# The router of a product-key expert layer: a second search over 112 sums in place of 256

## The chip, the cores and the metric

One Trainium2 chip, one of its cores. The metric is the time of one launch on the device in microseconds (us), the median over runs.

## The reference

One step of a one-layer decoder: attention and pooling, then an expert layer with product keys (PEER). The change touches only the choice of experts. For each of 1056 tokens (in 9 tiles of 128) and each of 8 heads:

```python
q = (hb @ w_pq).reshape(t, PEER_HEADS, 2, PEER_HALF)
s = jnp.einsum('thpk,hpnk->thpn', q, peer_keys).astype(jnp.float32)
sv, si = lax.top_k(s, PEER_TOPK)                        # 2 x (16 of 128 keys), sorted
cand = sv[:, :, 0, :, None] + sv[:, :, 1, None, :]      # 16 x 16 sums
cidx = si[:, :, 0, :, None] * N_KEYS + si[:, :, 1, None, :]
fv, fi = lax.top_k(cand.reshape(t, PEER_HEADS, 256), PEER_TOPK)
e = jnp.take_along_axis(cidx.reshape(t, PEER_HEADS, 256), fi, axis=-1)
g = jax.nn.softmax(fv, axis=-1)
```

The 16 experts `e` of a token and head are then evaluated and summed with the weights `g`.

## The kernel before

The program is a row of blocks, each with its own code for TensorE, VectorE, ScalarE, GpSimd and the DMA queue SyncE, and with a barrier of all engines at its end. `router` is such a block, and it is run twice: for the first 2 token tiles (names that begin with `t0`) amid the attention, and for the other 7 tiles (`t2`) after it. T is the number of tiles, and token is the partition. After the early router the kernel goes on with attention; after the late one `gate_matrix` spreads the gates, and a long stage of dense experts follows.

Inside a router the engines work through 8 heads. `heads` writes head 0 and head 7 out and rolls heads 1 to 6 into a loop. The parts of a head:

- ScalarE and GpSimd split the query weights of each half into a high and a low part (lines 1314 and 1364). GpSimd's split waits for ScalarE's.
- TensorE forms the queries in three products (lines 1276 to 1278) as soon as GpSimd's split is there, and with the keys the scores (line 1285). ScalarE copies both out (lines 1321 and 1329).
- VectorE finds the 16 best of each half (`top16`), writes the 256 sums (line 1439) over the scores, and finds the 16 best of these, again with `top16`. That function makes five passes over all the rows it is given: MAX8 (line 1409), FIND_INDEX8 (1413), MATCH_REPLACE8 (1417), MAX8 (1422), FIND_INDEX8 (1426); the find and replace passes have a MATCH_VALUE_LOAD before each. Between passes `settled` waits for the pass and copies one column (line 1403).
- VectorE then subtracts the best sum (line 1446), turns the place found (`at`, 0 to 255) into its row (shift by 4, line 1450) and column (and with 15, line 1451), casts both to float (1453), and compares each with 0 to 15 (line 1458, twice; the second comparison follows at once).
- GpSimd picks the key numbers by these comparisons: a multiplication (line 1380) and four halving sums (line 1386), for each half. In GpSimd's order of head m stand the two next splits and then the picks of head m-1. VectorE may cast the indices of head m (line 1438) only when the picks of head m-1 are done.
- ScalarE takes the exponential (line 1351) of head m-1 in the midst of head m; VectorE sums it, inverts it and writes the gates (lines 1462, 1464, 1466), which ends its head.

At the end VectorE forms the expert numbers for the gathered tiles (line 1473), and TensorE and ScalarE turn the picks of the others.

Of the kernel before, what the change touches and what calls it, by code (L numbers as in the profile page):

```python
# [9 lines left out]
U32 = mybir.dt.uint32  # L10
I32 = mybir.dt.int32
ALU = mybir.AluOpType
# [4 lines left out]
P = 128  # L17
# [24 lines left out]
NK = 128  # L42
HP = 16
TOPK = 16
TB = NT // 3
TA = 2
TG = 4
# [1138 lines left out]
def router(nc, a, t0, t1, queries_of, picks, gather, g0, g1):  # L1186
# [3 lines left out]
    with ExitStack() as ctx:  # L1190
        tag = f"t{t0}"
        T = t1 - t0
# [5 lines left out]
        def sb(name, shape, dt=F32):  # L1198
# [12 lines left out]
        idx = sb("c_idx", [P, T, 2, TOPK], U32)  # L1211
        idf = sb("c_idf", [P, T, 2, TOPK])
        best = sb("c_best", [P, T, TOPK])
        at = sb("c_at", [P, T, TOPK], U32)
        ab = sb("c_ab", [P, 2, T * TOPK], U32)
        abf = sb("c_abf", [P, 2, T * TOPK])
        eq = [sb(f"c_eq{k}", [P, T * TOPK, TOPK]) for k in range(2)]
        gate = sb("c_gate", [P, T, TOPK])
        out = sb("c_out", [P, 3, T, H * TOPK])
# [6 lines left out]
        s_b = [bank(f"r_s{c}") for c in range(BANKS)]  # L1226
        turn = [bank(f"c_turn{c}") for c in range(3)]
        s = with_sems(nc, ctx, """r_in r_win0 r_win1 r_wh r_wl r_q r_qev r_s r_sev
            r_zero c_pad c_m1 c_i1 c_r c_m2 c_i2 c_idf c_cand c_fm1 c_fi1 c_fr c_fm2 c_fi2 c_ab c_abf c_eq c_pk
            c_sub c_exp c_tot c_inv c_gate c_tr c_ev c_rows c_h2 c_scaled""", tag)  # L1230
        PICK = 5
        w_in = [s["r_win0"], s["r_win1"]]
# [158 lines left out]
        @block.vector  # L1391
        def _(dve):
            dve.memset(pad[:], 0.0).then_inc(s["c_pad"], 1)
            if FULL < WIDE:
                for e in range(2):
                    dve.memset(qT[e][:, FULL:WIDE], 0.0).then_inc(s["r_zero"], 1)
            dve.wait_ge(s["c_pad"], 1)
            dve.wait_ge(s["r_in"], 48)

            def settled(name, value):  # L1400

                dve.wait_ge(s[name], value)
                dve.tensor_copy(pad[:, 1:2], pad[:, 0:1])

            def top16(src, n, v, i, m, sems):

                m1, i1, r, m2, i2 = sems
                for q in range(n):
                    op = dve.max(v[:, q, 0:8], src[:, q, :])
                op.then_inc(s[m1], 1)  # L1410
                settled(m1, m + 1)
                for q in range(n):
                    op = dve.max_index(i[:, q, 0:8], v[:, q, 0:8], src[:, q, :])
                op.then_inc(s[i1], 1)
                settled(i1, m + 1)
                for q in range(n):
                    op = dve.match_replace(out=src[:, q, :], in_to_replace=v[:, q, 0:8], in_values=src[:, q, :],
                                           imm_value=NEG)
                op.then_inc(s[r], 1)
                settled(r, m + 1)  # L1420
                for q in range(n):
                    op = dve.max(v[:, q, 8:16], src[:, q, :])
                op.then_inc(s[m2], 1)
                settled(m2, m + 1)
                for q in range(n):
                    op = dve.max_index(i[:, q, 8:16], v[:, q, 8:16], src[:, q, :])
                op.then_inc(s[i2], 1)

            def first(m, e, late, last):
                cols = bass.ds(m * TOPK, TOPK)  # L1430
                st = scores[e][:].rearrange("p t k n -> p (t k) n")
                cand = scores[e][:].rearrange("p t k n -> p t (k n)")
                settled("r_sev", 2 * BANKS * m + 2 * BANKS)
                top16(st, 2 * T, val[:].rearrange("p t k i -> p (t k) i"), idx[:].rearrange("p t k i -> p (t k) i"),
                      m, ("c_m1", "c_i1", "c_r", "c_m2", "c_i2"))
                dve.wait_ge(s["c_i2"], m + 1)
                after(dve, s["c_pk"], 2 * PICK * m)
                dve.tensor_copy(idf[:], idx[:]).then_inc(s["c_idf"], 1)
                dve.tensor_tensor(cand.rearrange("p t (i j) -> p t i j", j=TOPK),
                                  val[:, :, 0, :].unsqueeze(3).to_broadcast((P, T, TOPK, TOPK)),  # L1440
                                  val[:, :, 1, :].unsqueeze(2).to_broadcast((P, T, TOPK, TOPK)),
                                  ALU.add).then_inc(s["c_cand"], 1)
                settled("c_cand", m + 1)
                top16(cand, T, best, at, m, ("c_fm1", "c_fi1", "c_fr", "c_fm2", "c_fi2"))
                after(dve, s["c_gate"], m)
                dve.tensor_tensor(gate[:], best[:], best[:, :, 0:1].to_broadcast((P, T, TOPK)),
                                  ALU.subtract).then_inc(s["c_sub"], 1)
                dve.wait_ge(s["c_fi2"], m + 1)
                flat = at[:].rearrange("p t k -> p (t k)")
                dve.tensor_scalar(ab[:, 0, :], flat, 4, None, ALU.logical_shift_right).then_inc(s["c_ab"], 1)  # L1450
                dve.tensor_scalar(ab[:, 1, :], flat, 15, None, ALU.bitwise_and).then_inc(s["c_ab"], 1)
                dve.wait_ge(s["c_ab"], 2 * m + 2)
                dve.tensor_copy(abf[:], ab[:]).then_inc(s["c_abf"], 1)
                dve.wait_ge(s["c_abf"], m + 1)
                dve.wait_ge(s["c_idf"], m + 1)
                for k in range(2):

                    dve.tensor_tensor(eq[k][:], abf[:, k, :].unsqueeze(2).to_broadcast((P, T * TOPK, TOPK)),
                                      iota[:, 0:TOPK].unsqueeze(1).to_broadcast((P, T * TOPK, TOPK)),
                                      ALU.is_equal).then_inc(s["c_eq"], 1)  # L1460
                dve.wait_ge(s["c_exp"], m + 1)
                dve.tensor_reduce(tot[:], gate[:], AX, ALU.add).then_inc(s["c_tot"], 1)
                dve.wait_ge(s["c_tot"], m + 1)
                dve.reciprocal(inv[:], tot[:]).then_inc(s["c_inv"], 1)
                dve.wait_ge(s["c_inv"], m + 1)
                dve.tensor_tensor(out[:, 0, :, cols], gate[:], inv[:].unsqueeze(2).to_broadcast((P, T, TOPK)),
                                  ALU.mult).then_inc(s["c_gate"], 1)
            heads(dve, first, lambda m, e: lambda: None)
            dve.wait_ge(s["c_gate"], H)
            G = g1 - g0  # L1470
            dve.tensor_copy(gather.gate[:, g0:g1, :], out[:, 0, 0:G, :]).then_inc(s["c_rows"], 1)
            dve.wait_ge(s["c_pk"], 2 * PICK * H)
            dve.scalar_tensor_tensor(out=gather.expert[:, g0:g1, :], in0=out[:, 1, 0:G, :], scalar=float(NK),
                                     in1=out[:, 2, 0:G, :], op0=ALU.mult, op1=ALU.add).then_inc(s["c_rows"], 1)
            dve.wait_ge(s["c_h2"], 16 * (G + 1))
            for g in range(g0, g1):
                dve.tensor_tensor(gather.y[g][:], gather.y[g][:], gain[:], ALU.mult).then_inc(s["c_scaled"], 1)
# [558 lines left out]
```

## Time and profile before

| what | us |
|---|---|
| median of 3 runs | 3992.42 |
| lowest and highest run | 3988.97, 4019.62 |
| profiled execution | 3987.4 |
| its span in the trace | 3985.6 |
| VectorE busy in the span | 3007.7 (75%) |
| TensorE busy in the span | 3195.7 (80%) |
| GpSimd busy in the span | 1578.3 (40%) |
| ScalarE busy in the span | 1041.1 (26%) |

The shares are means over stages that differ. In the profile DVE is VectorE, ACT is ScalarE, POOL is GpSimd, PE is TensorE and SP is SyncE; L1439 is line 1439 of the kernel. Lines that a helper records stand under the helper's line, and names without numbers (`t2r_scores`) stand for all buffers of a kind. The chain that ended last covers only the last 20 us of the program, and it says nothing about the routers; their stages are read from the windows and the timelines.

### The profile page before, as it was taken

What the parts mean: (1) busy time and instruction counts of PE and PEld (TensorE: products, weight loads), DVE (VectorE), ACT (ScalarE), POOL (GpSimd) and SP (SyncE); (2) the same over time, 40 slices, a digit from 0 to 9 for tenths busy, and PEclk for the clock granted to TensorE, in tenths of its full rate; (3) what the DMA queues carried; (4) which work ended last, traced back from release to release, by engine and by line L of the source; (5) the groups of instructions that cost most, each with busy time, mean ns of one, the idle gap of its engine ahead of it and who ended that gap; (6) DMA issues with size and microseconds to landing.
All of it is one profiled execution on the core that took longest, in us unless ns stands there. A gap on an engine that the chain in (4) does not pass through costs nothing. (4 is left out here: it accounts for less than half of the span.)

```text
span 3985.6 us, 57178 instructions
## 1 busy us (share of the span) xinstructions
PE 3195.7 (80%) x19892; PEld 2704.8 (68%) x19892; DVE 3007.7 (75%) x5897; ACT 1041.1 (26%) x1915; POOL 1578.3 (40%) x1320
## 2 busy tenths in 40 slices
PE   6654687776999986656552777999999999999997
PEld 3443344554555554336552667999999999999997
DVE  3248686885656663758998996888888888888887
ACT  2221122321222221111112553222222222223221
POOL 0035454464333332644545772333333333333332
PEclk9677897977889897778776888999999999999999
DMA  2221775687867655970000438888888888888886
GB/s 104 102 91 33 277 266 194 206 271 238 283 216 229 220 189 191 330 277 27 27 11 1 180 135 296 307 300 301 298 298 296 296 290 295 300 302 295 292 300 236
DMA packets 303822, 876.75 MB, mean 220 GB/s; under 512 B 34009, under 2 KB 125450, under 8 KB 292554
## 3 DMA queue, kind: packets, MB, share of 16 engines
q0 software_dynamic: 147456, 536.94, 39.5%
q1 hardware_dynamic: 154170, 334.15, 23.3%
q10 hardware_dynamic: 2016, 3.67, 0.3%
q8 instruction: 64, 1.05, 0.1%
q14 instruction: 116, 0.95, 0.1%
HBM read 819.17 MB, written 55.74 MB: 220 GB/s over the span
## 5 line engine op out<-in xcount | busy, mean ns | idle before, releaser
L109 POOL DMA_INDIRECT x_got<-v,x_expert x512 | 546.2, 1067 | 974.0 <-DVE x_y L130 874.3
L109 POOL DMA_INDIRECT x_got<-u_rows,x_expert x512 | 566.0, 1106 | 822.3 <-DVE x_got L123 703.5
L130 DVE SCALAR_TENSOR_TENSOR x_y<-x_got,x_hidden,x_y 128x1024 f32<-128x1024 f32 x512 | 665.9, 1301 | 40.8 <-DMA x_got<-v,x_expert 31.3
L123 DVE SCALAR_TENSOR_TENSOR x_got<-x_got,x_y 128x1024 f32<-128x1024 f32 x512 | 620.1, 1225 | 38.0 <-DMA x_got<-u_rows,x_expert 36.8
L1667 PE MATMUL e_a<-h2h,e_uh 128*128 128x272 f32 x2048 | 590.8, 288 | 22.1 <-DVE e_ul L1745 21.5
L1669 PE MATMUL e_a<-h2h,e_ul 128*128 128x272 f32 x2048 | 594.1, 290 | 0.0
L1684 PE MATMUL e_y<-e_wh,e_vh 128*128 128x272 f32 x2048 | 588.4, 287 | 3.6 <-DVE e_wl L1768 3.6
L1668 PE MATMUL e_a<-h2l,e_uh 128*128 128x272 f32 x2048 | 589.3, 288 | 0.0
L1685 PE MATMUL e_y<-e_wl,e_vh 128*128 128x272 f32 x2048 | 588.2, 287 | 0.0
L1686 PE MATMUL e_y<-e_wh,e_vl 128*128 128x272 f32 x2048 | 587.2, 287 | 0.0
L1667 PEld LDWEIGHTS e_a<-h2h,e_uh 128*128 128x128 f32 x2048 | 386.4, 189 | 22.9 <-issue 21.9
L1684 PEld LDWEIGHTS e_y<-e_wh,e_vh 128*128 128x128 f32 x2048 | 385.7, 188 | 3.8 <-issue 3.8
L1668 PEld LDWEIGHTS e_a<-h2l,e_uh 128*128 128x128 f32 x2048 | 386.9, 189 | 0.0
L1669 PEld LDWEIGHTS e_a<-h2h,e_ul 128*128 128x128 f32 x2048 | 385.7, 188 | 0.0
L1686 PEld LDWEIGHTS e_y<-e_wh,e_vl 128*128 128x128 f32 x2048 | 385.4, 188 | 0.0
L1685 PEld LDWEIGHTS e_y<-e_wl,e_vh 128*128 128x128 f32 x2048 | 385.1, 188 | 0.0
L759 PE MATMUL d_kn<-w_uk_kept,d_page 128*128 128x512 f32 x512 | 281.3, 676 | 11.3 <-DMA d_krT<-page_krT 5.3
L1713 ACT ACTIVATE e_vh<-e_v 128x2048 fp32r<-128x2048 f32 x64 | 122.2, 1909 | 632.9 <-PE e_y L1686 632.9
L1781 DVE TENSOR_TENSOR y<-e_y,y 128x272 f32<-128x272 f32 x496 | 214.0, 434 | 96.1 <-PE e_y L1686 95.6
L1516 DVE TENSOR_TENSOR g_hot<-g_iota,picks 128x1024 f32<-128x1024 f32 x136 | 230.4, 1769 | 4.2 <-DMA g_iota<-iota 4.2
L1539 PE MATMUL g_acc<-g_hot 128*128 128x128 f32 x1088 | 168.2, 317 | 67.9 <-POOL g_hot L1526 67.8
L1539 PEld LDWEIGHTS g_acc<-g_hot 128*128 128x128 f32 x1088 | 153.6, 224 | 82.7 <-POOL g_hot L1526 82.4
(376 smaller groups left out, 5681.4 us busy)
## 6 DMA issues: line engine op xcount, KB each, us to landing
e_u<-uT SPq DMA_DIRECT2D x128, 512.0 KB, 6.6
e_v<-v SPq DMA_DIRECT2D x64, 1024.0 KB
gates_d<-g_stage SPq DMA_DIRECT2D x8, 4352.0 KB, 11.8
e_gate<-gates_d SPq DMA_DIRECT2D x32, 1088.0 KB
d_page<-page SPq DMA_DIRECT2D x128, 144.0 KB, 2.3
d_latent<-page_rows SPq DMA_DIRECT2D x128, 128.0 KB
t0r_w<-w_pq SPq DMA_DIRECT2D x16, 512.0 KB, 3.5
x_got<-u_rows,x_expert POOLq DMA_INDIRECT x512, 5.6
```

The lines of the kernel that those rows point to most:

```text
L109: pool.indirect_dma_start(out=self.got[n % RING_G][:], out_offset=None, in_=self.tables[phase], in_offset=bass.IndirectOffsetOnAxis(ap=sel ...
L123: dve.scalar_tensor_tensor(out=row[:], in0=row[:], scalar=1.0, in1=self.y[g][:], op0=ALU.mult, op1=ALU.mult, accum_out=self.hidden[:, g, k ...
L130: dve.scalar_tensor_tensor(out=self.y[g][:], in0=row[:], scalar=self.hidden[:, g, k:k + 1], in1=self.y[g][:], op0=ALU.mult, op1=ALU.add).t ...
L759: pe.matmul(kn[p % 2][:, :], page[e][:, p, k * P:(k + 1) * P], w_uk[:, k, :], start=k == 0, stop=k == CT - 1)
L1516: dve.tensor_tensor(hot[q % RING][:], iota[:].unsqueeze(1).unsqueeze(1).to_broadcast((P, 2, GRP, NK)), picks[:, 1:3, GRP * q:GRP * (q + 1) ...
L1539: mm = pe.matmul(acc[q % RING][:, j * NK:(j + 1) * NK], hot[q % RING][:, 0, j, :], hot[q % RING][:, 1, j, :], start=True, stop=True)
L1667: pe.matmul(o, uh[q][:, k, :], h2h[:, k, cols], start=k == 0, stop=False)
L1668: pe.matmul(o, uh[q][:, k, :], h2l[:, k, cols], start=False, stop=False)
L1669: mm = pe.matmul(o, ul[q][:, k, :], h2h[:, k, cols], start=False, stop=k == KD - 1)
L1684: pe.matmul(o, h, wh[r][:, cols], start=c == 0, stop=False)
L1685: pe.matmul(o, h, wl[r][:, cols], start=False, stop=False)
L1686: mm = pe.matmul(o, l, wh[r][:, cols], start=False, stop=c == 3)
```

## The change

Of the 16 x 16 sums of two sorted lists, a sum in row i and column j (from 0) has at least (i+1)(j+1) - 1 sums that are not smaller. The 16 best can be found among those with (i+1)(j+1) <= 16. The kernel after takes rows 0 to 3 whole (64 sums) and 4 columns of rows 4 to 15 (48 sums), writes them next to each other in two additions, and searches 112 sums. The place found is turned back by arithmetic: row = max(place >> 4, (place >> 2) - 12), column = max(place - 16 row, place - 4 row - 48). The places now lie in the third row of `ab`, so one cast takes all three. The query, score, pick and exponential code is unchanged, as are the number and order of passes of `top16`.

```diff
+LONG, SHORT = 4, 4
...
-        at = sb("c_at", [P, T, TOPK], U32)
-        ab = sb("c_ab", [P, 2, T * TOPK], U32)
-        abf = sb("c_abf", [P, 2, T * TOPK])
+        ab = sb("c_ab", [P, 3, T * TOPK], U32)
+        at = ab[:, 2, :].rearrange("p (t k) -> p t k", k=TOPK)
+        abf = sb("c_abf", [P, 3, T * TOPK])
+        part = sb("c_part", [P, 2, T * TOPK])
...
-                cand = scores[e][:].rearrange("p t k n -> p t (k n)")
+                cand = scores[e][:].rearrange("p t k n -> p t (k n)")[:, :, 0:LONG * TOPK + (TOPK - LONG) * SHORT]
...
-                dve.tensor_tensor(cand.rearrange("p t (i j) -> p t i j", j=TOPK),
-                                  val[:, :, 0, :].unsqueeze(3).to_broadcast((P, T, TOPK, TOPK)),
-                                  val[:, :, 1, :].unsqueeze(2).to_broadcast((P, T, TOPK, TOPK)),
-                                  ALU.add).then_inc(s["c_cand"], 1)
-                settled("c_cand", m + 1)
+                for lo, hi, n, base in ((0, LONG, TOPK, 0), (LONG, TOPK, SHORT, LONG * TOPK)):
+                    dve.tensor_tensor(cand[:, :, base:base + (hi - lo) * n].rearrange("p t (i j) -> p t i j", j=n),
+                                      val[:, :, 0, lo:hi].unsqueeze(3).to_broadcast((P, T, hi - lo, n)),
+                                      val[:, :, 1, 0:n].unsqueeze(2).to_broadcast((P, T, hi - lo, n)),
+                                      ALU.add).then_inc(s["c_cand"], 1)
+                settled("c_cand", 2 * m + 2)
...
-                flat = at[:].rearrange("p t k -> p (t k)")
-                dve.tensor_scalar(ab[:, 0, :], flat, 4, None, ALU.logical_shift_right).then_inc(s["c_ab"], 1)
-                dve.tensor_scalar(ab[:, 1, :], flat, 15, None, ALU.bitwise_and).then_inc(s["c_ab"], 1)
+                dve.tensor_scalar(ab[:, 0, :], ab[:, 2, :], 4, None, ALU.logical_shift_right).then_inc(s["c_ab"], 1)
+                dve.tensor_scalar(ab[:, 1, :], ab[:, 2, :], 2, None, ALU.logical_shift_right).then_inc(s["c_ab"], 1)
                 dve.wait_ge(s["c_ab"], 2 * m + 2)
+                after(dve, s["c_place"], 3 * m)
                 dve.tensor_copy(abf[:], ab[:]).then_inc(s["c_abf"], 1)
                 dve.wait_ge(s["c_abf"], m + 1)
+                dve.scalar_tensor_tensor(out=abf[:, 0, :], in0=abf[:, 1, :], scalar=float(LONG - LONG * TOPK // SHORT),
+                                         in1=abf[:, 0, :], op0=ALU.add, op1=ALU.max).then_inc(s["c_row"], 1)
+                dve.wait_ge(s["c_row"], m + 1)
+                for k, n in enumerate((TOPK, SHORT)):
+                    dve.scalar_tensor_tensor(out=part[:, k, :], in0=abf[:, 0, :], scalar=float(-n), in1=abf[:, 2, :],
+                                             op0=ALU.mult, op1=ALU.add).then_inc(s["c_place"], 1)
+                dve.wait_ge(s["c_place"], 3 * m + 2)
+                dve.scalar_tensor_tensor(out=abf[:, 1, :], in0=part[:, 1, :], scalar=float(LONG * (SHORT - TOPK)),
+                                         in1=part[:, 0, :], op0=ALU.add, op1=ALU.max).then_inc(s["c_place"], 1)
+                dve.wait_ge(s["c_place"], 3 * m + 3)
                 dve.wait_ge(s["c_idf"], m + 1)
```

## Rows read from the trace of the kernel before

**Rows 1.** Windows: start:end, length, busy us (count) of PE, PEld, DVE, ACT, POOL, clock, DMA

```profile
210.00:397.00 187.00, 84.04 (x456) 78.92 (x456) 129.06 (x561) 34.12 (x62) 90.21 (x97) 0.71 0.19 66
1748.00:2158.00 410.00, 190.78 (x1392) 186.53 (x1391) 345.04 (x1527) 57.24 (x113) 189.38 (x105) 0.73 0.12 41
```

**Rows 2.** Line 1439: count, ns min/median/max, first and last start in us, form

```profile
L1439 DVE TENSOR_TENSOR t0r_scores<-t0c_val x8: 678/682/2831, 250.0 to 379.4; 128x512 f32<-128x512 f32 x8
L1439 DVE TENSOR_TENSOR t2r_scores<-t2c_val x8: 2016/2017/2022, 1820.1 to 2114.6; 128x1792 f32<-128x1792 f32 x8
```

**Rows 3.** Timeline of VectorE in a late head: start, us, instruction

```profile
1904.07 0.28 DVE L1438 CAST t2c_idf<-t2c_idx 128x224 f32<-128x224 uint32 x1
1904.26 2.02 DVE L1439 TENSOR_TENSOR t2r_scores<-t2c_val 128x1792 f32<-128x1792 f32 x1
...
1920.02 0.26 DVE L1446 TENSOR_TENSOR t2c_gate<-t2c_best 128x112 f32<-128x112 f32 x1
1920.20 0.21 DVE L1450 TENSOR_SCALAR t2c_ab<-t2c_at 128x112 uint32<-128x112 uint32 x1
1920.33 0.21 DVE L1451 TENSOR_SCALAR t2c_ab<-t2c_at 128x112 uint32<-128x112 uint32 x1
1920.57 0.28 DVE L1453 CAST t2c_abf<-t2c_ab 128x224 f32<-128x224 uint32 x1
1920.88 3.96 DVE L1458 TENSOR_TENSOR t2c_eq<-t2c_abf,t2r_iota 128x1792 f32<-128x1792 f32 x2
...
1925.40 3.43 DVE L1466 TENSOR_TENSOR t2c_out<-t2c_gate,t2c_inv 128x112 f32 x1
```

**Rows 4.** Groups of VectorE by form: busy us, mean ns, then idle time before

```profile
L1426 DVE FIND_INDEX8 t2c_idx<-t2c_val,t2r_scores 128x8 uint32<-128x128 f32 x112 | 29.4, 284 | 0.0
L1417 DVE MATCH_REPLACE8 t2r_scores<-t2c_val,t2r_scores 128x128 f32<-128x128 f32 x112 | 29.3, 275 | 0.0
...
L1422 DVE MAX8 t2c_val<-t2r_scores 128x8 f32<-128x128 f32 x112 | 22.4, 276 | 0.0
...
L1426 DVE FIND_INDEX8 t2c_at<-t2c_best,t2r_scores 128x8 uint32<-128x256 f32 x56 | 22.3, 420 | 0.0
L1417 DVE MATCH_REPLACE8 t2r_scores<-t2c_best,t2r_scores 128x256 f32<-128x256 f32 x56 | 22.2, 409 | 0.0
...
L1422 DVE MAX8 t2c_best<-t2r_scores 128x8 f32<-128x256 f32 x56 | 19.0, 410 | 0.0
...
L411 DVE SCALAR_TENSOR_TENSOR t2f_c<-t2f_zck,t2f_rstd,t2f_g_kv 128x256 f32<-128x256 f32 x7 | 3.4, 484 | 0.2
...
L1453 DVE CAST t0c_abf<-t0c_ab 128x64 f32<-128x64 uint32 x8 | 1.6, 194 | 0.3
...
L1473 DVE SCALAR_TENSOR_TENSOR x_expert<-t2c_out 128x256 uint32<-128x256 f32 x1 | 0.4, 426 | 10.5 <-POOL t2c_out L1386 10.5
```

**Rows 5.** Timeline of GpSimd around the same head, idle time before in brackets

```profile
1899.22 0.37 POOL L1386 TENSOR_TENSOR t2c_out<-t2c_eq 128x112 f32 x1 [0.19 <-POOL t2c_eq L1386]
...
1909.16 2.40 POOL L1364 TENSOR_TENSOR t2r_wl<-t2r_w,t2r_wh 128x1024 fp32r<-128x1024 f32 x1 [7.15 <-ACT t2r_wh L1314]
1922.99 5.72 POOL L1380 TENSOR_TENSOR t2c_eq<-t2c_eq,t2c_idf 128x1792 f32<-128x1792 f32 x1 [11.43 <-DVE t2c_eq L1458]
```

**Rows 6.** Timeline of ScalarE, the exponential of the same head

```profile
1920.31 0.30 ACT L1351 ACTIVATE t2c_gate<-t2c_gate 128x112 f32<-128x112 f32 x1 [4.63 <-DVE t2c_gate L1446]
```

**Rows 7.** Waits in the early router: us in total, times, longest

```profile
POOL t0c_eq L1380 <- DVE t0c_eq L1458: 13.8, 2, 7.1
...
DVE t0c_tot L1462 <- ACT t0c_gate L1351: 9.1, 4, 4.4
...
DVE t0c_idf L1438 <- POOL t0c_out L1386: 5.3, 4, 1.6
```

**Rows 8.** Timeline of GpSimd in the early router, two first multiplications of the picks

```profile
263.66 1.28 POOL L1380 TENSOR_TENSOR t0c_eq<-t0c_eq,t0c_idf 128x512 f32<-128x512 f32 x1
...
356.32 1.29 POOL L1380 TENSOR_TENSOR t0c_eq<-t0c_eq,t0c_idf 128x512 f32<-128x512 f32 x1
```

More of the change, by code:

```diff
@@ L1228, in router @@
         s = with_sems(nc, ctx, """r_in r_win0 r_win1 r_wh r_wl r_q r_qev r_s r_sev
-            r_zero c_pad c_m1 c_i1 c_r c_m2 c_i2 c_idf c_cand c_fm1 c_fi1 c_fr c_fm2 c_fi2 c_ab c_abf c_eq c_pk
+            r_zero c_pad c_m1 c_i1 c_r c_m2 c_i2 c_idf c_cand c_fm1 c_fi1 c_fr c_fm2 c_fi2 c_ab c_abf c_row c_place c_eq c_pk
             c_sub c_exp c_tot c_inv c_gate c_tr c_ev c_rows c_h2 c_scaled""", tag)
```

## The prediction

> **What bounds the kernel now.** I read the views from the coarse to the fine. The busy time by stage comes first: the changed code runs in two stages, the early router and the late router, and in the late one VectorE is busy 345.0 of 410 us while TensorE has 190.8, GpSimd 189.4 and ScalarE 57.2 [rows 1]. In the early one VectorE has only 129.1 of 187 us. So the two stages must be judged apart. The starts of line 1439, which runs once for each of the 8 heads, give the period of a head: (2114.6 - 1820.1) / 7 = 42.07 us late and (379.4 - 250.0) / 7 = 18.5 us early [rows 2]. The timeline of VectorE inside one late head shows the instructions end to end, with no wait in it [rows 3]. Its partners wait for it: GpSimd was idle 11.43 us until VectorE's first comparison of line 1458 [rows 5], ScalarE 4.63 us until line 1446 [rows 6]. The late router is therefore as long as VectorE's own list of instructions, and what leaves that list leaves the time. The two routers are blocks of their own with a barrier behind them, so what follows moves up whole; the last comparison is followed by the same work of GpSimd and TensorE as before.
>
> The early router is different. In its window VectorE waits four times for ScalarE's exponential (9.1 us) and four times for GpSimd's picks (5.3 us); only twice does GpSimd wait for VectorE, 13.8 us in all [rows 7]. The rest of that stage is a ring of GpSimd, TensorE and ScalarE: split the weights, multiply, copy out, split again, pick. Five turns of it last 356.32 - 263.66 = 92.7 us, 18.5 us each, the same as VectorE's period there [rows 8]. A faster VectorE will mostly wait longer in it.
>
> **What is removed, for each late head (7 token tiles).** The second search makes five passes over 7 tiles: two MAX8, two FIND_INDEX8, one MATCH_REPLACE8. Going from 128 to 256 columns lengthens them by 410 - 276 = 134, 420 - 284 = 136 and 409 - 275 = 134 ns [rows 4], so 1.05 ns a column. From 256 to 112 columns is 144 columns: 0.150 us less each, and 5 x 7 x 0.150 = 5.25 us. I extend the line by 16 columns below the shortest row; were 112 to cost no less than 128, the saving would be 35 x 0.134 = 4.69 us, which is its lower bound. The value loads in front and the five settling copies stay.
>
> The sums of line 1439: 512 columns take 0.682 and 1792 take 2.017 us [rows 2], so 0.148 us fixed and 1.043 ns a column. The two new adds have 7 x 64 = 448 and 7 x 48 = 336 columns: 0.615 and 0.498 us. Neighbours that don't wait for each other overlap by about 0.08 us (line 1451 begins 0.13 us after line 1450, which lasts 0.21 [rows 3]). So 2.017 falls to 0.615 + 0.498 - 0.08 = 1.03 us: 0.98 us saved. The second add has inner runs of 4 sums, which no row shows; at twice the price a column it would cost 0.35 us more, at its lower end it costs nothing more.
>
> **What is added, for each late head.** The bitwise-and becomes a shift of the same size: nothing. The cast grows from 224 to 336 columns; 64 cost 194 ns [rows 4] and 224 cost 276 ns [rows 3], 0.51 ns a column, so +0.06 us, and +0.23 us if the third row of the tile made it run at the 1.04 ns of the adds with its fixed part. Then come four SCALAR_TENSOR_TENSOR of 112 columns: one, two side by side, one, and each group waits for the one before. No row has this operation at 112 columns. At 256 it took 426 ns on line 1473 and 484 ns on line 411 [rows 4]; less 144 x 1.043 = 150 ns that is 276 or 334 ns. The plain two-input subtraction at 112 columns took 0.26 us and the one-input shift 0.21 [rows 3]. I take 276 ns, since line 1473 has the same form, a constant factor and two tensors in SBUF. An awaited neighbour starts about 0.03 us after the other ends: line 1453 at 1920.57 lasts 0.28, line 1458 begins at 1920.88 [rows 3]. So the chain is (0.276 + 0.03) + (0.276 - 0.08 + 0.276 + 0.03) + (0.276 + 0.03) = 1.11 us. At 0.21 us each it is 0.85, at 0.334 it is 1.34 us, and three register operations of 0.06 us for the new wait values may add 0.2; the present waits show no such gap.
>
> The Trainium skill speaks against such a chain: its page "VectorE: DVE Perf Modes", section "The TRN2 errata", says each instruction on SBUF pays a fixed latency, so that many small tiles pay it many times, and gives (N + 151) / 0.96 ns for an fp32 two-input add. That would be 274 ns at 112 columns, against the 0.26 us of the trace, and this estimate leaves the sum at 1.10 us. The same page's section on the DRAIN lets no operation start before the pipe is empty; lines 1450 and 1451 overlap here, and without overlap the chain would be an estimated 0.08 us dearer.
>
> **Net late.** 5.25 + 0.98 - 0.06 - 1.11 = 5.06 us a head, 8 heads: 40.5 us, and a period of 37.0 us. The lower corner is 4.69 + 0.63 - 0.23 - 1.54 = 3.55, or 28 us; with only the chain dear (1.34) and the rest as reckoned it is 4.83, or 39 us. The upper corner is 5.25 + 0.98 - 0.06 - 0.85 = 5.3, or 42.6 us.
>
> **Does cover run out there?** The work of each partner hangs on a point that moves with it. VectorE's line 1438 waits for the picks of the head before: they end at 1899.59 [rows 5] and it starts at 1904.07 [rows 3], 4.5 us of room. Both are counted from the last comparison, so that room stays. GpSimd's second split ends at 1909.16 + 2.40 = 1911.56, and its next work waits until 1922.99 [rows 5]; 5.06 us less leaves 6.4. ScalarE is ready 4.63 us before line 1446 is done [rows 6]; line 1446 comes 5.25 + 0.98 = 6.2 us earlier, so the exponential will now start about 1.6 us after it. VectorE asks for it only behind the chain and both comparisons, some 0.9 + 1.1 + 3.9 us later, so that is covered. GpSimd's shortest ring is 11.97 us from the end of the picks to the end of the second split, and 1899.59 - (1922.99 - 42.07) = 18.7 us of picks: 30.7 us, below 37.0.
>
> **Early router (2 token tiles).** A head saves 10 x 0.150 = 1.50 on the search and 0.68 - 0.45 = 0.23 on the sums (128 + 96 columns); it pays about 0.80 (steps of 32 columns at some 0.19 us, from the 0.194 us cast of rows 4). Net 0.9 us. For the first six heads the ring sets the pace: nothing. The last head's comparisons are waited for, 0.9 us of gain. VectorE will also reach its comparisons a little before GpSimd's second split rather than with it. The ring's splits and multiplies are stretched by such meetings now, and I allow 1 us; bounds for the whole early stage are -3 and +4 us.
>
> **Sum.** 40.5 + 0.9 + 1 = 42.4, say 42 us of the profiled execution: 3987.4 - 42 = 3945 us (its span 3985.6 to 3944). The median of the runs shown, 3992.4, is 5 us above the profiled one, so the median of after should be 3950 us. That is 1.05% faster, right beside the bound of 1% (39.9 us), which is about what a measurement of this kernel can tell from no change.
>
> **Rivals.**
> (a) The forecast, 40 to 46 us saved: 3946 to 3952. For it: rows linear in columns and no idle time on VectorE in the late head.
> (b) The same mechanism at its dear end: the chain at 334 ns an operation with register work, and the inner runs of 4 slow, 28 to 39 us saved: 3954 to 3964. For it: 4 to 5 dependent small operations have no exact row. Against it: the subtraction at 112 columns is short.
> (c) VectorE stops being the last: with the DVE period below GpSimd's ring of 31 us the rest of the gain would be lost. It decides only when more than 11 us a head are saved. A milder form is the early router's, where 7 x 0.9 = 6 us are given up already. A hidden ring in the late stage that kept the period at 40 us would give 16 us: 3976.
> (d) Slower: the shared port. Line 1466 took 3.43 us for 112 columns [rows 3] because it began inside GpSimd's multiplication, 1922.99 to 1928.71 [rows 5], and ended just behind it. Were the new operations to begin inside such instructions, each meeting would cost up to 2.4 us (a split) or 4 us (a multiplication). Two meetings a late head eat the 5.06 us; from there it is slower, and four (2 x 2.4 + 2 x 4 = 12.8 us) would add 8 x 7.7 = 62 us: 4054. Against it: GpSimd has nothing between 1911.56 and its wait for the comparison, and the new stretch lies at about 1914 to 1916 on that scale. The Trainium skill, page "SBUF — State Buffer", section "Who interferes with whom", says the same of a VectorE instruction with two SBUF inputs: it blocks against a GpSimd instruction that reads SBUF. By that rule, and the trace of line 1466 agrees, the two new adds and all four steps are exposed, where the searches are not.
>
> **Numbers.** (a) 0.57, (b) 0.36, (c) 0.05, (d) 0.02. The range 3938 to 3968 holds (a) and most of (b), with some us for the spread of runs (3989 to 4020). Faster by over 1%: 0.56, within: 0.42, slower: 0.02.
>
> **What would show it.** Starts of the sums 37.0 us apart late and 18 to 18.5 us early; the second search's MAX8 and FIND_INDEX8 near 0.26 and 0.27 us; new operations near 0.28 us with no outlier of 2 us; VectorE still without idle time in a late head; more waits for ScalarE and GpSimd early. A late period above 38 us, or any new operation of over 0.5 us, would make the prediction wrong.

## The result

| what | us |
|---|---|
| before, median of 14 runs (lowest to highest) | 4009.8 (3985.4 to 4021.1) |
| after, median of 14 runs (lowest to highest) | 3964.7 (3943.1 to 3983.6) |
| ratio of after to before, 95% interval | 0.9882 (0.9860 to 0.9905) |
| forecast for after, range | 3950 (3938 to 3968) |
| profiled execution of after, its span | 3975.4, 3973.6 |

The kernel after is 1.2% faster, 45 us between the medians. The forecast was 42 us, 1.05%.

The spans of the two profiled executions differ by only 12 us, 3985.6 against 3973.6. The stages, cut at the first VectorE instruction of each block, tell why. The rows are windows of after: start and end, length, busy us of TensorE, its weight loads, VectorE, ScalarE, GpSimd, then TensorE's granted clock and the DMA share. They are the early router, the attention block that follows it, and the late router.

```profile
219.70:393.70 174.00, 80.13 (x448) 75.57 (x448) 120.10 (x598) 31.66 (x59) 85.60 (x96) 0.72 0.20 64
393.70:977.60 583.90, 443.82 (x1599) 290.91 (x1599) 418.81 (x823) 152.94 (x325) 281.11 (x223) 0.75 0.69 232
1797.60:2147.10 349.50, 188.04 (x1391) 184.30 (x1391) 295.61 (x1559) 57.52 (x112) 181.02 (x96) 0.77 0.10 33
```

The same three stages of before:

```profile
219.50:396.90 177.40, 82.10 (x448) 77.35 (x448) 127.57 (x558) 31.62 (x59) 87.87 (x96) 0.72 0.19 63
396.90:947.90 551.00, 405.89 (x1599) 263.89 (x1599) 417.11 (x823) 154.16 (x325) 281.29 (x223) 0.81 0.73 246
1770.90:2158.70 387.80, 190.72 (x1391) 186.53 (x1391) 336.64 (x1520) 56.83 (x112) 180.44 (x96) 0.74 0.09 30
```

The late router went from 387.8 to 349.5 us and the early one from 177.4 to 174.0. The attention between them, of which no line was changed, took 583.9 us where it had taken 551.0, at a granted clock of 0.75 against 0.81. That takes back 33 us of the gain in this one pair of executions. The stretch between the attention and the late router gives the other 3 us (823.0 against 820.0). The experiments below show the same stage at both lengths for several kernels.

The head's period comes from line 1440 of after, the cast of the indices, once a head (count; ns min, median, max; first and last start):

```profile
L1440 DVE CAST t0c_idf<-t0c_idx x8: 195/1254/2351, 249.7 to 377.0; 128x64 f32<-128x64 uint32 x8
L1440 DVE CAST t2c_idf<-t2c_idx x8: 276/277/277, 1848.1 to 2108.1; 128x224 f32<-128x224 uint32 x8
```

Late: (2108.1 - 1848.1) / 7 = 37.14 us, against 42.07 by the first and last start in [rows 2]. Early: (377.0 - 249.7) / 7 = 18.19 us against 18.5. The timeline of VectorE in a late head answers to [rows 3] (start, us):

```profile
1894.84 0.26 DVE L1449 TENSOR_TENSOR t2c_gate<-t2c_best 128x112 f32<-128x112 f32 x1
1895.01 0.21 DVE L1452 TENSOR_SCALAR t2c_ab<-t2c_ab 128x112 uint32<-128x112 uint32 x1
1895.13 0.21 DVE L1453 TENSOR_SCALAR t2c_ab<-t2c_ab 128x112 uint32<-128x112 uint32 x1
1895.47 0.34 DVE L1456 CAST t2c_abf<-t2c_ab 128x336 f32<-128x336 uint32 x1
1895.84 0.28 DVE L1460 SCALAR_TENSOR_TENSOR t2c_abf<-t2c_abf 128x112 f32<-128x112 f32 x1
1896.15 0.46 DVE L1464 SCALAR_TENSOR_TENSOR t2c_part<-t2c_abf 128x112 f32<-128x112 f32 x2
1896.65 0.28 DVE L1467 SCALAR_TENSOR_TENSOR t2c_abf<-t2c_part 128x112 f32<-128x112 f32 x1
1896.96 3.96 DVE L1473 TENSOR_TENSOR t2c_eq<-t2c_abf,t2r_iota 128x1792 f32<-128x1792 f32 x2
...
1901.47 3.50 DVE L1481 TENSOR_TENSOR t2c_out<-t2c_gate,t2c_inv 128x112 f32 x1
```

The chain is the four new operations from 1895.84 to 1896.93, 1.09 us with its last gap to the comparisons 1.12. None of them waits for another engine. The operations in front and behind are as long as before, except the cast, 0.34 us where it was 0.28, and the multiplication of line 1481, 3.50 us where line 1466 took 3.43. The groups by form, which answer to [rows 4] (busy us, mean ns):

```profile
L1428 DVE FIND_INDEX8 t2c_ab<-t2c_best,t2r_scores 128x8 uint32<-128x112 f32 x56 | 13.9, 269 | 0.0
L1419 DVE MATCH_REPLACE8 t2r_scores<-t2c_best,t2r_scores 128x112 f32<-128x112 f32 x56 | 13.8, 260 | 0.0
...
L1424 DVE MAX8 t2c_best<-t2r_scores 128x8 f32<-128x112 f32 x56 | 10.6, 261 | 0.0
...
L1442 DVE TENSOR_TENSOR t2r_scores<-t2c_val 128x448 f32<-128x448 f32 x8 | 4.9, 618 | 0.0
...
L1442 DVE TENSOR_TENSOR t2r_scores<-t2c_val 128x336 f32<-128x336 f32 x8 | 4.0, 501 | 0.0
...
L1464 DVE SCALAR_TENSOR_TENSOR t2c_part<-t2c_abf 128x112 f32<-128x112 f32 x16 | 3.7, 271 | 0.3
...
L1456 DVE CAST t2c_abf<-t2c_ab 128x336 f32<-128x336 uint32 x8 | 2.7, 335 | 0.8
...
L1460 DVE SCALAR_TENSOR_TENSOR t2c_abf<-t2c_abf 128x112 f32<-128x112 f32 x8 | 2.2, 276 | 0.3
```

The passes over 112 sums take 269, 260 and 261 ns, 151, 149 and 149 less than over 256, so the line through 128 and 256 columns goes on to 112. The short inner runs of 4 cost nothing: 336 columns take 501 ns, where 498 were reckoned.

The waits of GpSimd and VectorE in the early router, against [rows 7] (us in total, times, longest):

```profile
POOL t0c_eq L1382 <- DVE t0c_eq L1473: 12.0, 2, 6.2
...
DVE t0c_tot L1477 <- ACT t0c_gate L1353: 10.0, 5, 3.9
...
DVE t0c_idf L1440 <- POOL t0c_out L1388: 7.8, 6, 1.6
```

VectorE waits for the exponential and for the picks 11 times instead of 8, for 17.8 us in all instead of 14.4.

### The profile page after: what moved, and what is told of

It is laid out like the page before. It is cut to its first block and busy times, and to the rows that moved or that the text cites. A ratio compares the mean times of both kernels' runs of the same rounds, so it can differ in the third digit from the quotient of the medians.

```text
span 3973.6 us, 57296 instructions
## 1 busy us (share of the span) xinstructions
PE 3224.3 (81%) x19892; PEld 2722.2 (69%) x19892; DVE 2961.7 (75%) x5977; ACT 1041.3 (26%) x1915; POOL 1579.9 (40%) x1320
## 3 DMA queue, kind: packets, MB, share of 16 engines
q0 software_dynamic: 147456, 536.94, 39.5%
q1 hardware_dynamic: 154170, 334.15, 23.4%
q8 instruction: 64, 1.05, 0.1%
```

## The experiments

The stages of every profiled execution, cut as above, in us; the period is that of a late head, from the cast of the indices:

| kernel | early router | attention | late router | late period | time of this execution |
|---|---|---|---|---|---|
| before | 177.4 | 551.0 | 387.8 | 42.07 | 3987.4 |
| after | 174.0 | 583.9 | 349.5 | 37.14 | 3975.4 |
| after, again | 173.8 | 554.4 | 348.3 | 37.14 | 3950.8 |
| search only | 172.4 | 573.5 | 339.4 | 35.89 | 3959.0 |
| decode only | 183.5 | 579.3 | 397.3 | 43.31 | 4031.8 |
| late router only | 176.6 | 553.4 | 348.2 | 37.14 | 3947.6 |
| early router, search only | 175.4 | 580.7 | 388.5 | 42.09 | 4010.0 |
| gates first | 184.1 | 574.0 | 347.8 | 37.01 | 3979.8 |
| late gate | 173.5 | 550.8 | 335.5 | 35.27 | 3934.1 |
| half searches | 170.9 | 577.0 | 295.3 | 31.69 | 3912.0 |
| late gate, unrolled | 177.0 | 550.4 | 332.8 | 34.80 | 3933.7 |

The rest moves less: from the end of the attention to the late router it is 818.4 to 825.6 us, in no order with the kernels, and from the end of the late router to the end of the program 1826.5 to 1828.9 us in all eleven. Of the kernels from search only to half searches, all but the late gate ran once, so their whole times can't be compared, only their stages.

**Search only.** The four steps of the chain are taken out of after.

```diff
-                dve.tensor_scalar(ab[:, 1, :], ab[:, 2, :], 2, None, ALU.logical_shift_right).then_inc(s["c_ab"], 1)
+                dve.tensor_scalar(ab[:, 1, :], ab[:, 2, :], 15, None, ALU.bitwise_and).then_inc(s["c_ab"], 1)
...
-                dve.tensor_copy(abf[:], ab[:]).then_inc(s["c_abf"], 1)
+                dve.tensor_copy(abf[:, 0:2, :], ab[:, 0:2, :]).then_inc(s["c_abf"], 1)
...
-                dve.scalar_tensor_tensor(out=abf[:, 0, :], in0=abf[:, 1, :], scalar=float(LONG - LONG * TOPK // SHORT),
...
-                dve.wait_ge(s["c_place"], 3 * m + 3)
```

> The kernel after without the four dependent steps that turn a place into a pair: 112 sums are searched, but the place is still cut with a shift by 4 and an and with 15, so for rows 4 to 15 the wrong experts are taken. Theory (VectorE alone sets the late router, and its costs add): a late head takes 42.07 - 5.25 - 0.98 = 35.8 us, 1.3 us below the 37.1 us of the kernel after. Rival (the steps of the chain lie in time that VectorE would have waited anyway): it stays at 37.1 us.

**Decode only.** The kernel before with the wider cast and the chain, on tiles that nothing reads.

```diff
-        ab = sb("c_ab", [P, 2, T * TOPK], U32)
-        abf = sb("c_abf", [P, 2, T * TOPK])
+        ab = sb("c_ab", [P, 3, T * TOPK], U32)
...
+        abf = sb("c_abf", [P, 3, T * TOPK])
...
+        extra = sb("c_extra", [P, 2, T * TOPK])
...
+                dve.scalar_tensor_tensor(out=extra[:, 0, :], in0=abf[:, 1, :], scalar=float(LONG - LONG * TOPK // SHORT),
+                                         in1=abf[:, 0, :], op0=ALU.add, op1=ALU.max).then_inc(s["c_row"], 1)
...
+                    dve.scalar_tensor_tensor(out=part[:, k, :], in0=extra[:, 0, :], scalar=float(-n), in1=abf[:, 2, :],
...
+                dve.scalar_tensor_tensor(out=extra[:, 1, :], in0=part[:, 1, :], scalar=float(LONG * (SHORT - TOPK)),
```

> The kernel before, searching 256 sums, with the wider cast and the four steps of the chain added; they write to a tile that nothing reads, so the result is that of before. Theory: a late head takes 42.07 + 0.06 + 1.11 + 0.1 for a register operation = 43.3 us, the late router 10 us more than before. Rival (shared port: the small two-input operations meet GpSimd at the moved phase): over 45 us, with single steps of 1 us and more. Together with the run without the chain the two must add up: 35.8 + 43.3 - 37.1 = 42.0 us.

The cast of the indices in the run without the chain, and in the one with nothing but the chain:

```profile
L1440 DVE CAST t2c_idf<-t2c_idx x8: 276/277/277, 1841.3 to 2092.5; 128x224 f32<-128x224 uint32 x8
```

```profile
L1441 DVE CAST t2c_idf<-t2c_idx x8: 276/277/278, 1854.8 to 2158.0; 128x224 f32<-128x224 uint32 x8
```

The periods are (2092.5 - 1841.3) / 7 = 35.89 and (2158.0 - 1854.8) / 7 = 43.31 us. So the search alone is worth 6.18 us a head and the chain costs 1.24 alone, 1.25 in after. The two runs add up to the kernel after: 35.89 + 43.31 - 37.14 = 42.06 against 42.07. VectorE's list is the whole of the late period, in both directions. A meeting with GpSimd stands in it, the 3.4 to 3.5 us of line 1466 or 1481, but it is in all four kernels and hardly changes, and no step of the chain met GpSimd in the late router. In the early router of decode only three steps did: they began inside a split and took 2.25 to 2.38 us where such a step takes 0.19, 6.4 us more in all. The rival's single steps of 1 us and more were there, in the stage that it was not written for.

**Late router only.** The early call goes to a copy of the router of before.

```diff
-                    router(nc, a, 0, TA, [(0, TA * P, (h2h, h2l), 0)], None, gather, 0, TA)
+                    router_before(nc, a, 0, TA, [(0, TA * P, (h2h, h2l), 0)], None, gather, 0, TA)
```

> The change is made in the late router alone; the early one is that of before. Theory: the early router takes 177 us as before and the late one 349 to 350 us as after, so all but 3 us of the gain is late. Rival (the early change moves the gathers and so the attention behind it): the stage from the start of the late attention block to the sample attention differs from the 551 us of before by more than its own scatter.

348.2 us late and 176.6 us early; the attention took 553.4. So the early change gives about 3 us and moves nothing behind it: the stage takes 177.4 and 176.6 us without the change and 174.0 and 173.8 with it, at a granted clock of 0.71 to 0.72 in all four.

**Early router, search only.** Late router as before; the early one searches 112 sums without the chain.

```diff
-                    router(nc, a, 0, TA, [(0, TA * P, (h2h, h2l), 0)], None, gather, 0, TA)
+                    router_short(nc, a, 0, TA, [(0, TA * P, (h2h, h2l), 0)], None, gather, 0, TA)
```

> The kernel before, but the early router searches 112 sums without the chain (and takes wrong experts for rows 4 to 15 there): VectorE's list shrinks by 1.7 us a head. Theory (a ring of GpSimd, TensorE and ScalarE sets the early router): it takes 173 to 175 us, no less than the 174.0 of the kernel after, and VectorE waits more. Rival (VectorE sets it there too): 177.4 - 8 x 1.7 = 164 us.

Waits in its early router:

```profile
DVE t0c_tot L1760 <- ACT t0c_gate L1647: 17.5, 6, 5.5
...
DVE t0c_idf L1734 <- POOL t0c_out L1682: 7.8, 6, 1.6
```

It took 175.4 us, 0.4 above the expected range, and the two waits grew from the 14.4 us of [rows 7] to 25.3. The search-only kernel has the same early router and took 172.4, so one such stage scatters by 3 us. The scatter goes with TensorE's granted clock, 0.68 here and 0.72 there: TensorE is busy 86.9 or 80.5 us with the same 448 matmuls. Both are on the side of the ring and far from 164: a shorter list turns into waiting. The other way it is not free. With the chain alone (decode only) the early router grew to 183.5, by 6.1 us. That is not the price of the chain alone: VectorE's busy time grew by 13.5 us, from 127.6 to 141.1, 6.4 of them from the three meetings with GpSimd, and its two waits fell from 14.4 to 6.4 us. In before, VectorE's list was close enough to the ring that a longer list soon sets the pace. The prediction's sentence that the ring sets the pace there holds for a shorter list only.

**Gates first.** Lines 1477 to 1481 of after are moved ahead of the comparisons.

```diff
-                dve.wait_ge(s["c_idf"], m + 1)
-                for k in range(2):
...
                 dve.wait_ge(s["c_exp"], m + 1)
                 dve.tensor_reduce(tot[:], gate[:], AX, ALU.add).then_inc(s["c_tot"], 1)
...
+                dve.wait_ge(s["c_idf"], m + 1)
+                for k in range(2):
```

> The kernel after with the sum, the inverse and the gates of a head (lines 1477 to 1481) moved ahead of the two comparisons of line 1473; the result is that of after. Theory of the shared port: line 1481 falls from 3.4 us to about 0.26 us in a late head, since GpSimd's multiplication has not begun. But VectorE now asks for the exponential before the comparisons, and ScalarE has it only some 16.4 us after the picks of the head before end, against the 12.1 us at which the chain would be done: a new wait of about 4 us, a late head of about 38 us and no gain. Rival (line 1481 is slow for its own pattern of 7 x 16 columns with a broadcast): it stays at 3.4 us, and a late head takes over 40 us.

Its groups of the sum, the gates and the cast of the indices (busy us, mean ns, idle time before and its releaser):

```profile
L1440 DVE CAST t2c_idf<-t2c_idx 128x224 f32<-128x224 uint32 x8 | 13.1, 1632 | 0.8
...
L1471 DVE TENSOR_REDUCE t2c_tot<-t2c_gate 128x7 f32<-128x112 f32 x8 | 2.2, 269 | 9.9 <-ACT t2c_gate L1353 9.8
...
L1475 DVE TENSOR_TENSOR t2c_out<-t2c_gate,t2c_inv 128x112 f32 x6 | 1.7, 275 | 2.0 <-DVE t2c_inv L1473 1.5
```

The multiplication fell from 3.47 us to 0.28, so its own pattern was never slow. The rival (own pattern) falls. What came in its place was only half foreseen. The wait for the exponential is 9.8 us over six heads, 1.6 us a head where 4 were expected. But the cast of the indices, now earlier, lasts 1.63 us in the mean and 2.26 at most instead of 0.28: it meets GpSimd's first split. The period is 37.01 us, not the 38 of the expectation, and the early router, where VectorE waited 20.5 us for the exponential, lost 10 us.

**Late gate.** Only line 1481 of after moves, into the next head behind the two additions.

```diff
-                dve.wait_ge(s["c_inv"], m + 1)
-                dve.tensor_tensor(out[:, 0, :, cols], gate[:], inv[:].unsqueeze(2).to_broadcast((P, T, TOPK)),
-                                  ALU.mult).then_inc(s["c_gate"], 1)
-            heads(dve, first, lambda m, e: lambda: None)
+
+            def tail(m, e):
+                def gates():
+                    dve.wait_ge(s["c_inv"], m + 1)
+                    dve.tensor_tensor(out[:, 0, :, bass.ds(m * TOPK, TOPK)], gate[:],
+                                      inv[:].unsqueeze(2).to_broadcast((P, T, TOPK)),
+                                      ALU.mult).then_inc(s["c_gate"], 1)
+                return gates
+            heads(dve, first, tail)
...
+                if late:
+                    late()
                 settled("c_cand", 2 * m + 2)
```

> The kernel after with the gates of head m-1 (line 1481 alone) written in head m, behind the two additions of the sums, where GpSimd has ended its first split and waits for ScalarE; the result is that of after. Theory of the shared port: line 1481 takes about 0.26 us, 3.2 us less; the cast of the indices comes earlier and meets that first split, which gives back some 0.7 us. A late head takes 34.6 us against 37.1, the late router some 20 us less than the 349.5 of after. The early router stays within 2 us of its 174. Rival (own pattern): 37.1 us and no gain.

The groups first, then the timeline of VectorE at the end of one head and the start of the next:

```profile
L1439 DVE CAST t2c_idf<-t2c_idx 128x224 f32<-128x224 uint32 x8 | 7.0, 879 | 0.8
...
L1485 DVE TENSOR_TENSOR t2c_out<-t2c_gate,t2c_inv 128x112 f32 x6 | 1.6, 264 | 0.0
```

```profile
1900.16 3.96 DVE L1474 TENSOR_TENSOR t2c_eq<-t2c_abf,t2r_iota 128x1792 f32<-128x1792 f32 x2
...
1904.33 0.20 DVE L1480 RECIPROCAL t2c_inv<-t2c_tot 128x7 f32<-128x7 f32 x1
1907.47 0.16 DVE L1405 COPY t2c_pad<-t2c_pad 128x1 f32<-128x1 f32 x1 [2.93 <-issue]
1907.54 2.80 DVE L1411 MAX8 t2c_val<-t2r_scores 128x8 f32<-128x128 f32 x14
```

The multiplication takes 264 ns and the cast 879, 0.6 us more, as expected. By these the period would be 34.5; it is 35.27. The missing 0.8 us are seen at 1907.47: 2.93 us in which VectorE waits for nothing that the profile shows, at a head that follows a turn back of VectorE's loop. The waits have it twice in the late router, 5.9 us, and 5.9 / 7 = 0.84. The trace shows VectorE's sequencer too, the part that carries out its waits, register operations and branches: it took the branch back at 1904.42, and its next register operation came 2.84 us behind that. In before and after the same place shows no idle time, but the sequencer has the same pause, 2.97 and 2.73 us in before and 2.76 and 3.01 in after; it began when line 1466 or 1481 had just begun, and their 3.4 us covered it.

**Late gate, unrolled.** VectorE's loop over heads 1 to 6 is written out. The cut is against the late-gate kernel.

```diff
-            heads(dve, first, tail)
+            first(0, 0, None, False)
+            for m in range(1, H):
+                first(m, m % 2, tail(m - 1, 1 - m % 2), m == H - 1)
+            tail(H - 1, 1)()
```

> The late-gate kernel with VectorE's loop over heads 1 to 6 written out; the other engines keep their loops, and the result is that of after. In the late-gate kernel VectorE stood idle for 2.93 us at the start of a head that follows a turn back of its loop, released by nothing. Theory (going back to the top of the loop costs VectorE about 3 us until the next instruction is there, which the stall of line 1481 had covered in before and after): the two turns of a router lose it, a late head takes 35.27 - 5.9 / 7 = 34.4 us, and the late router 6 us less than the 335.5 of the late-gate kernel. Rival (the first copy of a head waits for GpSimd's multiplication, whichever way the loop is written): it stays at 35.3 us. The early router stays at 174 us by both. The whole is about 26 us below the kernel after: some 3916 to 3922 us at the high clock of the attention block and 3944 to 3950 us at the low one.

VectorE's waits at a head's start in the late router, with the loop and without it:

```profile
DVE t2c_pad L1405 <- ACT t2r_scores L1331: 32.6, 2, 31.8
...
DVE t2c_pad L1405 <- issue: 5.9, 2, 2.9
```

```profile
DVE t2c_pad L1405 <- ACT t2r_scores L1331: 35.7, 6, 32.4
```

The idle time without a releaser is gone, so it belonged to the loop and not to GpSimd. The late period is 34.80 us, 0.4 above the theory and 0.5 below the rival. The gain is smaller than expected: 2.7 us late and not 6, since VectorE now waits 3.1 us more for ScalarE's scores and its casts of the indices take 1.2 us more, and 3.5 us are lost early. There the granted clock was 0.68 instead of 0.72 and TensorE busy 87.0 instead of 80.2 us, as in the slower of the two runs with the same early router above; that the loop has no part in it is not shown. The 6 runs took 3925.5 to 3938.2 and 3961.7 to 3967.3 us, above both ranges expected, with a median of 3950.0, no better than the late gate with its loop.

**Half searches.** The late-gate kernel, with the last three passes of each search left out and 8 values copied over the other 8.

```diff
-                for q in range(n):
-                    op = dve.match_replace(out=src[:, q, :], in_to_replace=v[:, q, 0:8], in_values=src[:, q, :],
...
+                dve.tensor_copy(v[:, :, 8:16], v[:, :, 0:8]).then_inc(s[m2], 1)
+                dve.tensor_copy(i[:, :, 8:16], i[:, :, 0:8]).then_inc(s[i2], 1)
```

> The late-gate kernel in which both searches find only 8 values and copy them over the other 8: the last three passes of each search are left out, so half of the experts are wrong. VectorE's list falls to about 34.6 - 10.2 - 5.0 = 19 us a late head. Theory (a ring of GpSimd, TensorE and ScalarE lies under VectorE): a late head takes 28.7 to 31 us, GpSimd waits for VectorE no more, and VectorE waits for the picks. Rival (no such ring, or one below 25 us): 19 to 25 us.

Its waits in the late router:

```profile
DVE t2c_pad L1405 <- ACT t2r_scores L1331: 47.1, 8, 31.9
...
DVE t2c_idf L1430 <- POOL t2c_out L1388: 34.5, 7, 8.4
POOL t2c_eq L1382 <- DVE t2c_eq L1465: 28.3, 6, 9.2
```

The head still takes (2049.3 - 1827.5) / 7 = 31.69 us, 0.7 above the expected range and far from the rival's. VectorE's list was reckoned at 19 us; in these seven heads VectorE is busy 23.4 us a head, since in the new place more of its operations meet GpSimd (a cast of the indices of 2.40 us, the two comparisons together 6.20 where 3.96 stood). VectorE waits 34.5 us for the picks, and behind the 31.9 us at the start it waits another 15.2 us for scores. So there is a floor under the late head, near the 30.7 us of the working and a little above it. That GpSimd "waits for VectorE no more" was wrong: it did so six times, 28.3 us in all. The floor is that of all four engines together, VectorE's stretched operations among them, and which of them sets it is not settled by this run. The sequencer's pause at the branch back is 0.23 and 0.26 us in this late router, and 0.26 to 0.31 us in the early router of before and after. A turn of those loops keeps VectorE busy with 174, 138 and 148 instructions, one of the late router of before and after with 378 and 388. So the long pause goes with the long loop; what makes it is not shown.

**After, again.**

> The kernel after, unchanged, run and profiled again beside the runs of before. Theory: the early router takes 174 us and the late one 349 to 350 us again, while the late attention block between them, whose code is the same in all kernels, takes anything from 551 to 584 us with TensorE's granted clock, so that single runs of one kernel differ by up to 35 us. Rival (the change itself makes the attention slower, 584 us against 551): it takes 580 us or more again.

The attention took 554.4 us this time and the two routers 173.8 and 348.3, so the rival is out. The stretch from 300 to 400 us behind the start of that block tells the two lengths apart. After, after again, and before:

```profile
693.70:793.70 100.00, 83.47 (x301) 59.41 (x300) 57.77 (x142) 27.16 (x65) 30.10 (x26) 0.58 0.45 137
```

```profile
692.60:792.60 100.00, 76.43 (x419) 55.08 (x417) 81.35 (x192) 38.02 (x86) 45.27 (x39) 0.91 0.64 207
```

```profile
696.90:796.90 100.00, 76.67 (x416) 54.84 (x415) 80.54 (x193) 37.66 (x85) 44.77 (x39) 0.90 0.66 205
```

The granted clock is 0.58 in one execution of after and 0.91 in the other, and TensorE gets through 301 or 419 matmuls in the 100 us. Over the eleven executions the clock in this stretch is 0.90 or 0.91 when the attention took 550 to 554 us, and 0.57 to 0.65 when it took 573 to 584 us, in every one. The change does not decide it: after has both lengths, and so have kernels with the late router of before.

## Why the prediction was right

**The bound.** It named VectorE's list as the late router's length. The two half changes add up to 0.01 us, so this is shown.

**Removed.** Each pass 0.150 us shorter (measured 0.149 to 0.151), the sums 0.98 us shorter (0.618 + 0.501 - 0.08 = 1.04 us where 2.02 stood). The search-only run gives 6.18 us where 6.23 stood.

**Added.** The four operations of 276, 271, 271 and 275 ns are what line 1473 had promised; the price by line 411, 334 ns, was too high. The chain was reckoned at 1.11 us and took 1.12. The cast took 335 ns against 276 + 60. What was missing is a gap of 0.12 us in front of that cast (1895.34 to 1895.47 in the rounded rows), where 0.03 had been taken: the new wait on `c_place` at 3 m stands there. With line 1481 at 3.47 instead of 3.42 us that makes 0.14 us, beside the 0.13 between the 5.06 of the sum and the measured 4.93 us a head. The cause is the register operation for the wait's value. In after the gap is 0.12 us in the six heads of the loop, with a register operation of 40 ns inside it at 1895.39, and 0.03 in heads 0 and 7, which are written out. In the unrolled kernel, where the value is a constant in every head, it is 0.03 us in all eight, and the idle time in front of the cast falls from 0.8 us to 0.3:

```profile
L1457 DVE CAST t2c_abf<-t2c_ab 128x336 f32<-128x336 uint32 x8 | 2.7, 335 | 0.3
```

The prediction had allowed up to 0.2 us for this and left it out of the sum, because the waits of before showed no such gap. Its trace had one elsewhere: 0.15 us in front of line 1466 (line 1464 begins at 1925.05 and lasts 0.20, line 1466 begins at 1925.40), with a register operation of 64 ns in it. Of the section on the DRAIN the prediction left out the end: that section of the Trainium skill, page "VectorE: DVE Perf Modes", goes on to say that an operation that is not held starts earlier. So it was here: the two of line 1464, of 271 ns each, take 0.46 us together.

**Cover.** ScalarE had the exponential at 1895.78, before the comparisons began, and line 1477 did not wait for it. The split of GpSimd ended before the new operations began. GpSimd waited 7.56 us for the comparisons of this head, where 6.4 had been reckoned, and line 1440 never waited for the picks in a late head.

**Early router.** 1.9 us were reckoned and 3.4 and 3.6 measured in two executions of after. VectorE waits more there, as foreseen. That the ring alone sets the pace was half right: decode only lengthened the stage by 6.1 us, in part through meetings with GpSimd. If the last head gave its 0.9, the ring became some 2.5 us shorter where I had allowed 1; the rows don't tell the two apart.

**The sum.** 42 us forecast; 38.3 + 3.4 = 41.7 us in the two routers of the first pair, 39.5 + 3.6 = 43.1 in the second execution. Between the medians of 14 runs it is 45 us, with an interval of the ratio from 38 to 56 us, so the sum and the measurement agree. Two misses cancel in it in part: the late router gave 38.3 and 39.5 us of the 40.5 reckoned, the early one 1.5 and 1.7 us more than its 1.9.

**The forecast time.** 3950 us was 15 us too low, for a reason that was not seen. The range's width held it, 3 us from its end, and that is luck in part. The 5 us that I added for the median came from three runs. In 14 runs of before 6 lie from 3985 to 3995 us (mean 3990.6) and 8 from 4008 to 4021 (mean 4015.1); in 14 of after 6 lie from 3943 to 3950 (3946.3) and 8 from 3963 to 3984 (3974.7). The six shorter ones of after are exactly those with a mean granted clock of 0.880 or more. Level by level the change is worth 44.3 and 40.4 us. The profiled execution of before and two of the three runs shown were of the group with the higher clock, and the sum started from there. The step that failed is the last one, from the profiled execution to the median: 5 us were added, and with 14 runs the median of before lies 22 us above its profiled execution.

**The rivals.** The dear end of the chain is out by the rows. That the chain would meet GpSimd on the port did not happen in after, but the mechanism is real: taking line 1481 out of GpSimd's multiplication made it 3.2 us shorter, and moving the cast into GpSimd's split made it up to 2 us longer. The chain itself met a split in two other kernels, three times in the early router of decode only (2.25 to 2.38 us instead of 0.19) and once in the late one of the half searches (2.49 instead of 0.27), at about the 2.4 us of the prediction. So the phase in which the chain runs spared it, as the prediction reckoned for the late router; for the early one it had not looked. The floor under VectorE exists, at 31.7 us or below, and only a saving of 10 us a head would have met it.

**A faster version.** The late gate does all the work of after and takes the late router from 348.3 to 335.5 us. On the same chip as after it ran 3934.1, 3935.8, 3962.1 and 3964.3 us against 3946.8, 3950.8, 3970.7 and 3978.2. By rank that is 12.7, 15.0, 8.6 and 13.8 us less, in line with the 12.8 us of the stage; the ratios to before, 0.9861 (0.9787 to 0.9934) and 0.9888 (0.9814 to 0.9963), are too wide to part them.

## What to carry to other kernels

Where one engine's timeline is full and all others wait for it, price the change from slopes and fixed parts of the rows; they held here to a few per cent, for the operation without a row of its own too, where of two rows (276 and 334 ns) the one with the same form was taken. Then look at what an instruction of that engine waits for inside its own duration: the 3.4 us of line 1481 stood in no list of waits, and moving it by one stage won a third of what the whole change did. A loop's way back can hide in the same place: look at the sequencer's rows, too. Before an effect of 1% is read from one pair of executions, compare stages that nothing was changed in; here one of them moved by 33 us.

## What was not expected of the hardware

- The granted clock of TensorE takes one of two courses in the same stretch of the same program: 0.90 to 0.91 or 0.57 to 0.65 over 100 us. With the second the attention is 19 to 34 us longer, of 550 to 554; TensorE is then busy for more of the time (83.5 against 76.4 us of 100) and does fewer matmuls (301 against 419). Before and after both come to it from a lull: TensorE was busy 29.4 of 50 us at a clock of 0.51 in before (650 to 700 us) and 30.2 of 50 at 0.57 in after (647 to 697). In the next 50 us the clock was 0.91 in before and 0.50, its lower level of 1.2 GHz, in after. What decides between them was not tested.
- A turn back of the late loop on VectorE cost 2.9 us of idle time once no stall stood before it, and nothing that could be seen in the waits while one did. The sequencer's pause behind the branch was 2.7 to 3.0 us where a turn held 378 or 388 instructions, and 0.2 to 0.3 us where it held 138 to 174.
- A two-input operation of 112 columns on VectorE lasts 3.4 to 3.5 us when it begins inside GpSimd's multiplication and 0.26 to 0.28 us otherwise. A cast of 224 columns lasts 0.28 us, or up to 2.40 us when it meets GpSimd's split; searches of the same tiles never changed their duration beside GpSimd (MAX8 over 128 columns, for one: 267 to 285 ns beside it and 268 to 284 alone in after). The Trainium skill, page "SBUF — State Buffer", section "Who interferes with whom", says that an operation with two SBUF inputs contends with GpSimd's reads and that a cast can; the traces agree.
